# A mixed attention-and-gates loop: head copies prepared two steps later, and each gate chunk placed first in its step

## The reference, cut to what matters

```python
ya = window_attention_latent(apply_rope(qa), apply_rope(ka), va, kac, vac, sink)   # 8 heads
yb = full_attention_latent(apply_rope(qb), apply_rope(kb), vb, kbc, vbc)           # 8 heads
x = x + gt1 * merge_branches(ya, yb, ga, gb, w_proj_a, w_proj_b, w_out)
# merge_branches: m = sigmoid(ga) * (ya @ w_pa) + sigmoid(gb) * (yb @ w_pb); return m @ w_o
...
if not last:   # layer 0 only: the context tokens attend to the context keys
    yac = context_attention(qac, kac, vac, N_KV_A, sink)
    ybc = context_attention(qbc, kbc, vbc, N_KV_B, None)
```

## Time and profile before

| | |
|---|---|
| time, median of 3 runs | 2522.95 us (2522.46 to 2525.45) |
| the profiled execution | 2522.46 us, of which 2520.7 us is its span |
| PE busy | 2372.5 us, 94% of the span |
| DVE busy | 1538.7 us, 61% |
| ACT busy | 1110.0 us, 44% |
| loop of layer 0, step 0 to the end of the steps | from 180.4 to 479.6 us |
| loop of layer 1, step 0 to the end of the steps | from 1318.2 to about 1542 us |

### The profile page before, as it was taken

One profiled execution on the slowest core, in us unless ns is written; L12 is line 12 of the kernel. 1 busy time (PEld: TensorE's weight loads), 2 busy tenths in 40 slices (PEclk: granted clock), 3 DMA queues, 4 the chain that ended last, 5 costly groups with the idle time before them and its releaser, 6 DMA issues.

```text
span 2520.7 us, 32132 instructions
## 1 busy us (share of the span) xinstructions
PE 2372.5 (94%) x12095; PEld 1987.2 (79%) x12095; DVE 1538.7 (61%) x2348; ACT 1110.0 (44%) x1755; POOL 145.6 (6%) x260
## 2 busy tenths in 40 slices
PE   7999999898899999999899998989999989888898
PEld 3888878787788888888778876878888868777687
DVE  5666767789555555544686776543333555378763
ACT  4447777622421121122647775342222454555541
POOL 0100000111000000000100001000000010000010
PEclk8999999999899999999899999989999989999899
DMA  5311111364333333322221113422222334321153
GB/s 234 118 63 46 52 38 51 117 239 167 112 131 134 134 129 122 121 88 84 92 83 52 51 51 127 141 75 98 95 94 98 109 113 140 135 77 60 67 198 111
DMA packets 67808, 267.68 MB, mean 106 GB/s; under 512 B 8416, under 2 KB 8480, under 8 KB 66512
## 3 DMA queue, kind: packets, MB, share of 16 engines
q1 hardware_dynamic: 42336, 162.94, 18.5%
q0 software_dynamic: 25328, 102.77, 11.5%
HBM read 237.37 MB, written 27.26 MB: 105 GB/s over the span
## 4 chain that ended last, share of the span: by engine, by line
PE 72%; DVE 13%; ACT 6%; issue 5%; DMA 3%; SPq 0%; POOL 0%; ACTq 0%; DVEq 0%; POOLq 0%
PE ps L186 20%; PE ps L187 19%; PE ps L188 19%; DVE wt_out L317 2%; DVE w_lo L182 1%; DMA w_raw<-in_stream 1%; PE ps L1062 1%; PE ps L1063 1%; PE ps L1064 1%; PE ps L996 1%; ACT w_hi L175 1%; PE ps L1003 1%; DMA ada_raw<-in_ada 1%; DVE inv L1248 1%; PE ps L1045 1%
## 5 line engine op out<-in xcount | busy, mean ns | idle before, releaser
L186 PE MATMUL ps<-h_hi,w_hi 128*128 128x512 f32 (+1 forms) x2328 | 860.3, 370 | 46.3 <-DVE h_lo L1342 15.1
L187 PE MATMUL ps<-h_lo,w_hi 128*128 128x512 f32 (+1 forms) x2328 | 846.2, 363 | 0.0
L188 PE MATMUL ps<-h_hi,w_lo 128*128 128x512 f32 (+1 forms) x2328 | 844.0, 363 | 0.0
L186 PEld LDWEIGHTS ps<-h_hi,w_hi 128*128 128x128 f32 x2328 | 444.7, 191 | 125.3 <-issue 28.8
L182 DVE TENSOR_TENSOR w_lo<-w_raw,w_hi 128x1024 fp32r<-128x1024 f32 x288 | 352.0, 1223 | 245.8 <-ACT w_hi L175 245.3
L188 PEld LDWEIGHTS ps<-h_hi,w_lo 128*128 128x128 f32 x2328 | 443.7, 191 | 70.7
L187 PEld LDWEIGHTS ps<-h_lo,w_hi 128*128 128x128 f32 x2328 | 444.6, 191 | 68.8 <-issue 2.4
L175 ACT ACTIVATE w_hi<-w_raw 128x1024 fp32r<-128x1024 f32 x288 | 302.9, 1053 | 311.2 <-PE ps L188 297.7
L187 PE MATMUL ps<-q_lo,w_hi 128*128 128x512 f32 x720 | 254.8, 354 | 0.0
L188 PE MATMUL ps<-q_hi,w_lo 128*128 128x512 f32 x720 | 254.3, 353 | 0.0
L186 PE MATMUL ps<-q_hi,w_hi 128*128 128x512 f32 x720 | 253.3, 352 | 0.2 <-DVE q_lo L1357 0.2
(11 more groups left out here) (333 smaller groups left out, 2915.0 us busy)
## 6 DMA issues: line engine op xcount, KB each, us to landing
w_raw<-in_stream SPq DMA_DIRECT2D x288, 512.0 KB, 3.2
wt<-in_ada_t POOLq DMA_DIRECT2D x80, 512.0 KB, 3.6
ada_raw<-in_ada SPq DMA_DIRECT2D x4, 2048.0 KB, 18.1
x_keep<-x POOLq DMA_DIRECT2D x8, 768.0 KB, 6.9
gates<-th_g POOLq DMA_DIRECT2D x16, 384.0 KB, 2.9
x<-x_keep POOLq DMA_DIRECT2D x2, 3072.0 KB, 13.3
gates<-sg POOLq DMA_DIRECT2D x24, 256.0 KB, 2.3
gates<-th_g POOLq DMA_DIRECT2D x16, 256.0 KB, 2.3
```

The lines of the kernel that those rows point to most:

```text
L186: nc.tensor.matmul(out_ap, lh, rh, start=start, stop=False)
L187: nc.tensor.matmul(out_ap, lh, rl, start=False, stop=False)
L188: return nc.tensor.matmul(out_ap, ll, rh, start=False, stop=stop)
```

## The change

Two lines of `attention_and_gates` are changed; it is used by both layers.

```diff
-            prep_at = [max(-PRO, tile_at[tiles.index((parts * h, 0))] - 4) for h in range(len(heads))]
+            prep_at = [tile_at[tiles.index((parts * h, 0))] - 2 for h in range(len(heads))]
             assert prep_at[0] == -PRO
...
                     todo = list(chunks_at(t))
-                    now = todo if t == -PRO else [q for q in todo[:1] if q % CH]
+                    now = todo if t == -PRO else todo[:1]
                     for q in now:
                         gate_chunk(q)
```

## The result

The change makes the kernel slower by 0.67%: 1.0067 times before, 95% interval 1.0051 to 1.0083 (median 2538.87 us over 13 runs against 2523.01 over 13). That is 17 us, with 13 to 21 in the interval; 19.3 was forecast. The profiled execution took 2543.19 us (forecast 2541.8), 2541.4 of them its span.

A forecast was written before the change was run, and what follows sets the result against it. PE, busy 2372.5 of 2520.7 us, was taken to bound the kernel. Terms 7.1 + 5.9 + 1.6 + 4.8 + 5.4 - 5.5 = 19.3 on 2522.46 gave 2541.8, stated as 2542 us; whole range 2518 to 2559.

The forecast's parts named there:

- Branch A in layer 0: First tiles of heads 1 to 8: PE waits about 1.2 us each for ACT's late second copy; +7.1 us net.
- The three things given back: Old layer 0 waits expected to go: sums 1.4, exponential 1.0, about 1.0 around 310 us; 3.4 us taken off.
- Branch B in layer 0: Later heads of layer 0, no sink: PE waits 0.45 us or more for the second copy; +5.9 us net.
- Chunk 0 ahead, layer 0: A gate unit's first chunk, moved ahead of the tile, waits longer for the previous unit's tanh; +1.6 us.
- ACT in layer 1: Copies at phases 4 and 5 end late for the first tile, more with tanh or weight split there; +4.8 us.
- DVE in layer 1: DVE's prep waits for the later copy and delays reciprocals and maxima, 0.9 us for each of six heads; +5.4 us.
- Won in layer 1: Phases 2 and 3 freed of copies, last maximum no longer behind DVE's prep, chunk 0 covering waits; -5.5 us.
- The rule on the clock: Both loops: by the skill, frequent PE pauses drop the clock; the forecast instead took gaps to cost only their length.
- that rival: The clock falls in the loops: 5 us a lapse, eight lapses 40 us, giving 2582 us; chance 0.03.
- In time after all: At each head's first tile the copies are ready and only the relief is left: 2512.5 us; chance 0.17.
- Won and lost cancel: Layer 1 wins, and layer 0's new stalls replace old waits almost one for one: about 2524 us; chance 0.15.
- The chain in DVE: DVE's delay carries into later heads, 1.7 us for seven heads in both layers, 18 us more: 2560 us; chance 0.09.

The follow-up runs named there:

- after_again: The changed kernel run once more, unchanged, for its profile; loops of 310.4 us in layer 0 and 227.7 us in layer 1.
- prep_only: The changed kernel with the old line for the chunks, so only the copies come two steps later; 1.0119 times before.
- chunk_only: The kernel before with only the new line for the chunks (chunk 0 ahead), copies still four steps ahead; 0.9984 times before.
- remainder_later: The changed kernel with DVE's subtraction (the remainder of a head) one step after the first copy; 1.0062 times before.
- before_again: The kernel before run again, unchanged, for its profile; loops of 296.3 us in layer 0 and 223.1 us in layer 1.

## Why the prediction was right, step by step

- **PE bounds the kernel, and a late copy is its time.** Right. The wait of line 1045 for line 1118 is there, in the heads where it was worked out. Forecast were 20 to 25 waits of about 15 us in all; the profile lists 12 in layer 0 and 4 in layer 1, 18.7 us. Three heads of layer 0 (first tiles in steps 2, 10 and 98) wait for the tanh ahead of the tile and not for the copy. In layer 1 there are delays that it does not list: step 36 is 0.5 us longer with no wait in the list.
- **Branch A in layer 0, +7.1.** The steps up to 62, without step 37, are 6.8 us longer. The single case was met to 0.1 (1.27 for 1.2). The three things given back came: steps 56 and 57 are 1.6 shorter, as ACT is no longer behind there.
- **Branch B in layer 0, +5.9.** In after_again, which has no lapse in this loop, 14.2 less 6.8 less 1.6 (next point) leaves 5.8. In the first profile it is 2.9 more, by two lapses. That the sum was met to 0.1 is in part luck. The worked case, head 14, was right (step 106 is 0.5 longer, 0.45 forecast), but steps 82 and 90 are 2.2 and 2.35 longer for 1.25 and 1.45 forecast, and steps 74 and 98, where a tanh or weight split was counted, 0.7 and 0.5 for 1.25 each.
- **Chunk 0 ahead, layer 0, +1.6.** As a cost beside the copies it is met: steps 37, 63 and 107 have grown by 0.9, 0.35 and 0.4. Alone it is 1.2. But the forecast had no term for what it spares when the copies are late (7.8 us in the two profiles, 3.6 without the lapses); it had it hidden in the heads, where a tile was always worked out behind its chunk. The sum was right for the whole change; its terms did not hold for either half alone. Without this term it is 17.7, and prep_only's loops are 30.9 longer (about 22.5 without lapses); the term itself is 1.6, and chunk_only's loops are 0.1 shorter.
- **ACT in layer 1, +4.8.** Eight steps with the first tile (36 to 84) have grown by 5.6; step 48, with tanh and weight split in the two steps before, by 1.9.
- **DVE in layer 1, +5.4.** This term was too large. What is left of the 6.0 after the 5.6 above and the 4.6 won is 5.0, of which one lapse of the clock (after a wait of 2.1 us for a maximum in step 43) is 1.4; 3.6 remain. By remainder_later about 1.0 of it is DVE's standing (2.4 less the lapse, which that profile does not have). If the lapse comes from the longer wait in step 43, which all four profiles allow, it belongs here too. The rest would be the subtraction itself, ahead of the divisions; that was not tried by itself and is not shown.
- **Won in layer 1, -5.5.** The steps that are shorter (8, 16, 21, 28, 40, 73, 82, 86) make 4.6; step 28 alone 1.5, where PE waited for the exponential.
- **The rule on the clock, and that rival.** I took it from a single execution that gaps as long leave the clock alone. That was wrong: before_again has a lapse after the same gap. The rival named from the Trainium skill, "TensorE: Matmul & The Clock Gate", section "A second HAM failure mode: psum-queue depth-cycling", happened in part. Here a gap costs about 1.4 us more than its length in some of the cases where it reaches 1.7 to 2.5 us; I had priced a lapse at 5 from the opening of layer 1. It is 4.3 of the 23.1 us of the profiled execution, and the sum had it at nothing.
- **The sum.** 19.3 were forecast; both loops are 23.1 us longer, 20.2 in after_again. The measured ratio gives 16.9, interval 12.9 to 20.9. The profiled loops lie near or above its upper end, so how well the 19.3 is met can't be told closer than some 3 us. The rest of the kernel differs by up to 22 us from one profile to another, and no profile here says whether the difference is chance or something that the change returns.
- **The rivals.** In time after all: refuted by the first row of waits. Won and lost cancel: true of layer 1 only for copies three steps ahead (221.1 for 221.7). The chain in DVE: its upper bound was far off.

## What to carry over

In a loop written out by hand, a task moved to a later step meets what stands in its new steps: work out when the engine is through with those steps already, beside the time at which the reader comes, and if the two are within the length of the task there is no slack (278.55 against 278.32 here). Averages would have said the opposite, as ACT had 22% of its time free. Work of the bounding engine that needs nothing, put just ahead of a wait, is worth more the later the awaited thing is, so two edits of this kind can't be costed apart. And where the whole kernel's time scatters by 0.7% (2512 to 2529 us here), the length of the loop in the trace tells 0.2 us, once the lapses of the clock in each profile have been counted: two readings above had to be cut down by more than half for one lapse.

## What the runs showed of the hardware

- A gap of 1.67 us in PE's work left the granted clock at 1.00 in two executions of one kernel and was followed by a short lapse to the 1.2 GHz level in a third, with the same 8.3 us busy of ten. The lapse cost 1.4 us. With the gaps of 1.96 and 2.46 us it came in three and in two of four executions. A gap of 2.1 us had it four times of four in one place (step 43 of layer 1) and never in five in another (step 34 of layer 0).
- A stall of PE shows in the list of waits some 0.2 us shorter than it is (1.08 us listed, step 1.27 longer), and one of about 0.2 us may not show at all.
- But for those lapses the loops repeat to 0.2 us from one execution to the next (296.2, 296.3, 296.3), whereas the rest of the kernel, which has its openings and streams, varies by up to 22 us (1987 to 2009).
